# Expert outputs of a mixture-of-experts layer: a scatter by matmul per job, or a store per job and one gather per token

## Chip, cores and metric

The kernel runs on one core of one Trainium2 chip. The metric is the device time of one execution in microseconds (us). Before the change it is 1543.35 us, the median of three runs (1543.27 to 1545.74).

## What is computed

A decoder trunk of two layers on 256 tokens of 1024 channels, in float32. Layer 0 is a pooling and gating mixer, followed by a dense SwiGLU feed-forward (hidden size 2816). Layer 1 is an RWKV-7 time mixing, followed by the mixture of experts that the change touches; a last RMSNorm with a gain ends the kernel. The experts' part:

```python
def moe_swiglu(xn, router, wg, wu, wd):
    logits = xt.astype(F32) @ router.astype(F32)
    top_vals, top_idx = lax.top_k(logits, TOP_K)          # TOP_K = 2 of 8 experts
    top_w = jax.nn.softmax(top_vals, axis=-1)
    gates = jnp.sum(jax.nn.one_hot(top_idx, N_EXPERTS, dtype=F32) * top_w[..., None], axis=1)
    for e in range(N_EXPERTS):                            # D_FF_EXPERT = 3584
        out = out + gates[:, e:e + 1] * swiglu(xt, wg[e], wu[e], wd[e]).astype(F32)
```

## The kernel before

**Two halves of every weight.** Matrix products run in float32r with both factors split in a high and a low part. A weight piece of 128x1024 is copied to `w_hi` by ScalarE (L1635), and VectorE writes the rest, piece minus `w_hi`, to `w_lo` (L1731). TensorE then makes three products for each (L1531 to L1533). `w_hi` and `w_lo` hold four pieces each, so ScalarE writes piece n+4 only when TensorE has used piece n. The dense feed-forward of layer 0 does the same with `f_hi` (L2042) and `f_lo` (L2153).

**Jobs.** The router picks two experts for each token. Tokens are sorted by expert with a one-hot matrix and ranks; an expert with more than 128 tokens gets a second job, so there are 8 to 11 jobs, and the trace has 8 (56 loads of each of the three weights, seven in a job). Job 0 is written out, the others run in a loop (`Fori(1, J)`) on each engine. A job takes up to 128 token rows, in slots of its own, and goes through seven chunks of 512 hidden columns: gate product, up product, SiLU times up, transposes (L1549), down product into PSUM banks 4 and 5. One chunk has three loads of 2 MB ("g", "u", "d"), 21 in a job, each in four pieces, so 84 pieces in a job. The names `i` and `j` in the code are the load within a job and the job.

**How rows get in.** The normed token rows are scattered once to a scratch tensor in memory, `expert_rows`, at row 128*expert + rank, by four indirect DMAs of GpSimd (L1919); `row_at` holds those rows. Each job reads its 128 rows from there (L1466), and TensorE turns them (L1567). The scratch is cleared at the start from `zero_rows`, 8 MB issued on SyncE (SP) after chunk 0 of the dense feed-forward (L1964).

**How outputs get out, before the change.** A job's output, 128x1024 in PSUM banks 4 and 5, is scaled by the gates of its rows and split in `Yhi` (ScalarE, L1653) and `Ylo` (VectorE, L1842). TensorE multiplies it by a one-hot matrix `PT` (8 products, L1579 and L1580, `scattered`), which gives 256 token rows in four banks, and VectorE adds these to `h` (four additions, L1835). This is done in the next job, behind its first gate product, and for the last job at the end. `PT` and the gates come from `Pg`, made by `onehot` on VectorE (L1818; for job 0 L1778), turned by two transposes on TensorE (L1594) and read at L1884 and L1885.

**Order around the change.** SP's loads of experts follow one another through a ring of seven slots; load i+7 waits until load i has been split (`free`). In the dense feed-forward SP loads 11 chunks of 3 MB through four slots. Chunk 3 waits for the first residual sum, and before chunk 4 SP runs `rwkv_lora_sp` (L549), which waits for the first clear (`x_clear`) and issues nine small loads. ScalarE starts on a chunk only when its three loads have all landed (L2039). At the end, ScalarE and VectorE take the norm of `h` and the rows are stored.

Of the kernel before, what the change touches and what calls it, by code (L numbers as in the profile page):

```python
# [105 lines left out]
def trunk(nc, I, cst_dram, cols_dram, out, stop=None):  # L106
    ctx = ExitStack()
    with ctx:
# [84 lines left out]
        n_r = sem("norm_recip")  # L193
        n_tr, n_eva, n_evd = sem("norm_transposed"), sem("norm_cols_act"), sem("norm_cols_dve")
        dvc = sem("dve_chain")
        acc_ = sem("act_chain")
        plc = sem("pool_chain")
        p_in, a_ev, g_ev = sem("in_proj"), sem("pool_in_copied"), sem("gelu_done")
        z_pad = sem("pads_zeroed")
        s_pooled, s_ymm, s_yev = sem("pooled"), sem("pool_mm"), sem("pool_out")  # L200
# [31 lines left out]
        f_phi, f_plo, f_pc = sem("ffn_pieces_hi"), sem("ffn_pieces_split"), sem("ffn_pieces_used")  # L232
        s_out = [sem(f"out{i}_written") for i in range(3)]

        chain = {"dve": 0, "act": 0, "pool": 0}
        CH = {"dve": dvc, "act": acc_, "pool": plc}

        def link(eng, which, ins):

# [309 lines left out]
        def rwkv_lora_sp(sp):  # L549
            sp.wait_ge(s_h, 4)  # L550
            sp.wait_ge(x_clear, 16)
            one = lambda name: I[name].rearrange("a (k p) n -> p (a k) n", p=P)
            two = lambda name: I[name].rearrange("a k n -> (a k) n")
            g2 = two("o_g2")
            for dst, src in ((w1s, one("o_w1")), (a1s, one("o_a1")), (g1s, one("o_g1")), (w2s[0:64, :], two("o_w2")),
                             (w2s[64:65, :], I["o_w0"]), (a2s[64:P, :], two("o_a2")), (g2a, g2[0:P, :]),
                             (g2b[0:32, :], g2[P:160, :]), (hspread, cst_dram[:, HSPREAD_AT:HSPREAD_AT + 1024])):
                sp.dma_start(dst, src).then_inc(lora_in, 16)
# [816 lines left out]
        def rwkv_pool(pool):  # L1375
# [19 lines left out]
        rows_dram = nc.dram_tensor("expert_rows", (2 * NE * P, D), F32).ap()  # L1395
        ng_in = sem("ffn_norm_gain_in")
        x_zero, x_clear, x_at, x_put, x_in = (sem(x) for x in (
            "zero_rows_set", "expert_rows_cleared", "row_index", "rows_scattered", "expert_rows_in"))
        zero_rows = wu(5, 1024, 1024)
        rows_in = xn[:, 0:D]  # L1400
        spare = xnT[:, :, :].rearrange("p k t -> p (k t)")
# [42 lines left out]
        def moe_sp(sp):  # L1444
            sp.wait_ge(o_mm, 56)
            sp.dma_start(router, I["o_router"].rearrange("a (k p) e -> p (a k) e", p=P)).then_inc(r_w, 16)
            wg = I["o_moe_wg"].rearrange("a e (k p) f -> (a e) p k f", p=P)
            wup = I["o_moe_wu"].rearrange("a e (k p) f -> (a e) p k f", p=P)
            wd = I["o_moe_wd"].rearrange("a e (k p) n -> (a e) p k n", p=P)

            def load(i, e):
                what, c = LOADS[i]
                if what == "d":
                    src = wd[bass.ds(e, 1), :, 4 * c:4 * c + 4, :]
                    dst = slot(SLOTS[i % 7]).rearrange("p (k n) -> p k n", k=4)
# [12 lines left out]
            def free(i, j):  # L1468

                sp.wait_ge(m_lo, j * NP + 4 * (i + 1))  # L1470

            for i in range(NL):
                if i == 0:
                    sp.wait_ge(l_xu, lev(1, 1, 1))
                if i == 1:
                    sp.wait_ge(t_u, 4)
                if i == 2:
                    sp.wait_ge(t_y, 4)
                if i == 4:
                    sp.wait_ge(gn_sp, 2)  # L1480
                    sp.wait_ge(wo_done, 4)
                if i >= 7:
                    free(i - 7, 0)
                load(i, 0)
                if i == 14:
                    sp.wait_ge(r_jobs, 2)
                    sp.dma_start(gain, I["final_norm"].partition_broadcast(P)).then_inc(r_in, 16)
                    sp.wait_ge(x_put, 64)
                    rows(0)
            J = sp.value_load(jobs[0:1, 12:13], min_val=NE, max_val=NE + 3)  # L1490
            with sp.Fori(1, J) as j:
                e = sp.value_load(jobs[0:1, bass.ds(j + 16, 1)], min_val=0, max_val=NE - 1)
                for i in range(NL):
                    free(i - 7, j)
                    load(i, e)
                    if i == 14:
                        rows(j)

# [9 lines left out]
        def moe_pe(pe):  # L1508
# [60 lines left out]
                    if k % 4 == 3:  # L1569
                        last.then_inc(m_ga, 1)  # L1570

            def scattered(j):

                pe.wait_ge(m_pte, j)
                pe.wait_ge(m_yl, j * 2)
                for b in range(TB):
                    for q in range(2):
                        dst = psum[:, 6 - 2 * q + b, :]
# [4 lines left out]
            def job(j, first):  # L1583
                pe.wait_ge(m_xg, j + 1)
                for c in range(NEC):
                    hidden(j, 0, c)
                    if c == 0 and not first:
                        scattered(j)
                    if c == 1:
                        if not first:  # L1590
                            pe.wait_ge(s_h, j * 4 + 12)
                        pe.wait_ge(m_pg, j + 1)
                        for b in range(TB):
                            last = nc.tensor.transpose(psum[:, 7, b * P:(b + 1) * P], Pg[:, b * P:(b + 1) * P], ident)  # L1594
                        last.then_inc(m_pt, 1)
# [5 lines left out]
                    if c == NEC - 1:  # L1601
                        down(j, c - 1, (0, 1))
                        turned(j, c)
                        down(j, c - 1, (2, 3))
                    elif c >= 1:
                        down(j, c - 1)
                down(j, NEC - 1)

# [2 lines left out]
            J = pe.value_load(jobs[0:1, 12:13], min_val=NE, max_val=NE + 3)  # L1611
            with pe.Fori(1, J) as j:
                job(j, False)
            scattered(J)

        def moe_act(act):
            act.wait_ge(gn_sp, 2)
# [31 lines left out]
            def outputs(j):  # L1649

                act.wait_ge(m_pc, j * NP)
                for q in range(2):
                    nc.scalar.activation(Yhi[:, 512 * q:512 * q + 512], psum[:, 4 + q, :], ACT.Copy,  # L1653
                                         scale=gate).then_inc(m_yc, 1)
# [25 lines left out]
            with act.Fori(1, J) as j:  # L1680
                job(j, False)
            root_table()
            outputs(J)
            for b in range(TB):
                for q in range(2):
                    act.wait_ge(s_h, J * 4 + (9 + 2 * b + q))
                    n = 2 * b + q
                    nc.scalar.activation(xn3[:, b, 512 * q:512 * q + 512], h[:, b, 512 * q:512 * q + 512], ACT.Square,
                                         accum_out=small[:, 104 + n:105 + n]).then_inc(n_ss, 1)
# [29 lines left out]
        def moe_dve(dve):  # L1719
# [54 lines left out]
            go(V.tensor_tensor(oh2, oh2, wide("w2"), ALU.mult))  # L1774
            V.tensor_tensor(gt[:, :, NE:2 * NE], oh1, oh2, ALU.add)
            go(V.tensor_tensor(gt[:, :, 0:NE], oh1, oh2, ALU.add))
            for b in range(TB):
                last = V.tensor_scalar(Pg[:, b * P:(b + 1) * P], C("iota"), rk[:, b, 0:1], gt[:, b, 0:1], ALU.is_equal, ALU.mult)  # L1778
            last.then_inc(m_pg, 1)

            A_, B_, O_ = tb_["ova"], tb_["ovb"], tb_["ovc"]

# [43 lines left out]
                                           xg_split[:, 0, 4 * q:4 * q + 4, :].bitcast(F32), ALU.subtract)  # L1826
                last.then_inc(m_xg, 1)

            def scattered(j, o=0):

                for b in range(TB):
                    for q in range(2):
                        dve.wait_ge(m_sc, j * 4 + (4 * o + 2 * b + q - 3))
                        hs = h[:, b, 512 * q:512 * q + 512]
                        V.tensor_tensor(hs, hs, psum[:, 6 - 2 * q + b, :], ALU.add).then_inc(s_h, 1)  # L1835

            def outputs(j, o=0):

                dve.wait_ge(m_xg, j + (o + 1))
                for q in range(2):  # L1840
                    dve.wait_ge(m_yc, j * 2 + (2 * o + q - 1))
                    V.scalar_tensor_tensor(out=Ylo[:, 512 * q:512 * q + 512], in0=psum[:, 4 + q, :], scalar=gate,  # L1842
                                           in1=Yhi[:, 512 * q:512 * q + 512].bitcast(F32), op0=ALU.mult,
                                           op1=ALU.subtract).then_inc(m_yl, 1)
# [6 lines left out]
            def job(j, first):  # L1851
# [7 lines left out]
                for i, (what, c) in enumerate(LOADS):  # L1859
# [8 lines left out]
                        pieces_lo(j, i, (1, 2, 3))  # L1868
                    elif not first or i > 0:
                        pieces_lo(j, i)  # L1870
                    if i == 0 and not first:
                        outputs(j)
                    if (what, c) == ("u", 0) and not first:
                        scattered(j)
                    if (what, c) == ("u", 1) and first:
                        job_list()
                    if what == "u" and c >= 1:
# [1 line left out]

                    if i >= 1 and LOADS[i - 1][0] == "u" and LOADS[i - 1][1] < NEC - 1:  # L1880
                        gated(LOADS[i - 1][1])
                    if (what, c) == ("d", 1):
                        dve.wait_ge(m_pt, j + 1)
                        V.tensor_reduce(gate, psum[:, 7, 0:256], AX.X, ALU.add)  # L1884
                        V.tensor_scalar(PT[:, :], psum[:, 7, 0:256], 0.0, None, ALU.is_gt).then_inc(m_pte, 1)  # L1885
                    if (what, c) == ("d", 3):
                        nxt = dve.value_load(jobs[0:1, bass.ds(j + 1, 1)], min_val=0, max_val=2 * NE - 1)
                        onehot(nxt)

            job(0, True)  # L1890
            J = dve.value_load(jobs[0:1, 12:13], min_val=NE, max_val=NE + 3)
            with dve.Fori(1, J) as j:
                job(j, False)
            last_job = dve.value_load(jobs[0:1, 13:14], min_val=NE - 1, max_val=NE + 2)
            outputs(last_job, 1)
            scattered(last_job, 1)

            dve.wait_ge(r_in, 16)
            for b in range(TB):
# [14 lines left out]
        def moe_pool(pool):  # L1914
# [3 lines left out]
            for i in range(2 * TB):  # L1918
                nc.gpsimd.indirect_dma_start(rows_dram, bass.IndirectOffsetOnAxis(row_at[:, i:i + 1], 0), xn3[:, i % TB, :],  # L1919
                                             None).then_inc(x_put, 16)  # L1920
        y_done = sem("y_done")


# [3 lines left out]
        def _(sp):  # L1927
# [16 lines left out]
            for c in range(NFC):  # L1944
# [17 lines left out]
                if c == 0:  # L1962
                    sp.wait_ge(x_zero, 1)
                    sp.dma_start(rows_dram.rearrange("(n p) d -> p n d", p=P),  # L1964
                                 zero_rows.unsqueeze(1).to_broadcast([P, 2 * NE, D])).then_inc(x_clear, 16)
            if reached(3):
                rwkv_sp(sp)
                wo_sp(sp)
# [415 lines left out]
```

## Time and profile before

| | us |
|---|---|
| Median of three runs | 1543.35 |
| Profiled execution, first to last instruction (span) | 1541.7 |
| What lies outside the span, by the median | 1.65 |
| TensorE busy | 1512.7 (98%) |
| VectorE busy | 1268.4 (82%) |
| ScalarE busy | 1009.2 (65%) |
| GpSimd busy | 9.3 (1%) |

The profile is of one execution. PE is TensorE, PEld its weight loads, DVE VectorE, ACT ScalarE, POOL GpSimd, SP SyncE, and a q behind a name its sequencer. Times in its rows are microseconds from the first instruction. The granted clock is a share of TensorE's full 2.4 GHz, so 0.50 is 1.2 GHz. "DMA share" is the mean busy share of the 16 DMA engines, slightly over 1 where packets overlap. "Busy" of a matmul includes its pipeline, so the distance from one start to the next is what a matmul costs.

### The profile page before, as it was taken

Reading aid. Unit: us, or ns where it says so; the run is one execution under the profiler, and the core shown is the slowest. Engines: PE = TensorE matmul, PEld = TensorE weight load, DVE = VectorE, ACT = ScalarE, POOL = GpSimd, SP = SyncE. Lnnn points to the kernel's source line nnn. Section 1 sums busy time; section 2 is a strip of 40 time slices with the busy share of each in tenths; the row PEclk is TensorE's granted clock in tenths of the full one; section 3 lists DMA queues with packets and bytes.
Section 4 is the critical chain, followed back from the end, with each engine's and each line's share of the span. In section 5 each row is a group of like instructions: output and inputs, shape, how many; then the busy total and the mean of one; then the engine's idle time right before and its main releaser. Section 6 shows DMA issues by size and latency. Waiting matters only on the chain.

```text
span 1541.7 us, 21572 instructions
## 1 busy us (share of the span) xinstructions
PE 1512.7 (98%) x7854; PEld 1265.2 (82%) x7854; DVE 1268.4 (82%) x1442; ACT 1009.2 (65%) x1154; POOL 9.3 (1%) x10
## 2 busy tenths in 40 slices
PE   8999999999999999999999999999999999999997
PEld 5788888799899677888888888888888888888885
DVE  3756666767875269999999999999999999999997
ACT  3444444653523157878887888887878888887886
POOL 0000000000000010000000000000000000000000
PEclk9999999999999999999999999999999999999999
DMA  9789443034004479999999999999999999999970
GB/s 361 309 268 298 164 164 109 0 110 136 1 1 165 178 266 396 397 375 357 386 365 361 386 363 362 387 359 360 384 381 345 379 381 348 376 380 347 375 288 27
DMA packets 203269, 439.36 MB, mean 285 GB/s; under 512 B 7217, under 2 KB 44337, under 8 KB 203090
## 3 DMA queue, kind: packets, MB, share of 16 engines
q1 hardware_dynamic: 200434, 434.05, 77.0%
q10 hardware_dynamic: 2208, 2.50, 0.5%
q0 software_dynamic: 576, 2.10, 0.3%
q8 instruction: 36, 0.59, 0.2%
q14 instruction: 15, 0.12, 0.0%
HBM read 427.09 MB, written 11.53 MB: 285 GB/s over the span
## 4 chain that ended last, share of the span: by engine, by line
PE 95%; DVE 3%; ACT 1%; issue 1%; DMA 0%; DVEq 0%; ACTq 0%
PE psum L1531 20%; PE psum L1533 19%; PE psum L1532 19%; PE psum L2313 5%; PE psum L590 5%; PE psum L2315 3%; PE psum L2237 2%; PE psum L879 2%; PE psum L2277 2%; PE psum L2279 2%; PE psum L2278 2%; PE psum L1549 2%; PE psum L775 1%; PE psum L765 1%; PE psum L680 1%; PE psum L2230 1%
## 5 line engine op out<-in xcount | busy, mean ns | idle before, releaser
L1731 DVE TENSOR_TENSOR w_lo<-ring,w_hi 128x1024 fp32r<-128x1024 f32 x672 | 805.5, 1224 | 51.3 <-ACT w_hi L1635 11.0
L1635 ACT ACTIVATE w_hi<-ring 128x1024 fp32r<-128x1024 f32 x672 | 711.4, 1062 | 187.0 <-PE psum L1533 186.9
L1531 PE MATMUL psum<-w_hi,xg_split 128*128 128x512 f32 x896 | 353.6, 395 | 0.4 <-DVE xg_split L1825 0.4
L1533 PE MATMUL psum<-w_lo,xg_split 128*128 128x512 f32 x896 | 349.5, 390 | 0.0
L1532 PE MATMUL psum<-w_hi,xg_split 128*128 128x512 f32 x896 | 348.9, 389 | 0.0
L1533 PEld LDWEIGHTS psum<-w_lo,xg_split 128*128 128x128 f32 x896 | 168.2, 188 | 35.7
L1531 PEld LDWEIGHTS psum<-w_hi,xg_split 128*128 128x128 f32 x896 | 168.3, 188 | 34.1 <-DVE xg_split L1825 0.6
L1532 PEld LDWEIGHTS psum<-w_hi,xg_split 128*128 128x128 f32 x896 | 168.5, 188 | 33.5
L1531 PE MATMUL psum<-w_hi,ht_split 128*128 128x512 f32 x448 | 176.2, 393 | 1.7 <-DVE w_lo L1731 1.7
L1533 PE MATMUL psum<-w_lo,ht_split 128*128 128x512 f32 x448 | 174.6, 390 | 0.0
L1532 PE MATMUL psum<-w_hi,ht_split 128*128 128x512 f32 x448 | 174.4, 389 | 0.0
L2313 PE MATMUL psum<-x_split,f_hi 128*128 128x512 f32 x352 | 125.1, 399 | 0.8 <-DVE x_split L357 0.4
L2153 DVE TENSOR_TENSOR f_lo<-ring,f_hi 128x1024 fp32r<-128x1024 f32 x66 | 79.5, 1223 | 52.0 <-ACT f_hi L2042 52.0
L2042 ACT ACTIVATE f_hi<-ring 128x1024 fp32r<-128x1024 f32 x66 | 69.0, 1056 | 53.6 <-PE psum L2315 31.3
L1531 PEld LDWEIGHTS psum<-w_hi,ht_split 128*128 128x128 f32 x448 | 84.1, 188 | 21.1 <-issue 4.0
L2315 PE MATMUL psum<-x_split,f_lo 128*128 128x256 f32 x352 | 98.9, 281 | 0.0
L1533 PEld LDWEIGHTS psum<-w_lo,ht_split 128*128 128x128 f32 x448 | 84.1, 188 | 17.8
L1532 PEld LDWEIGHTS psum<-w_hi,ht_split 128*128 128x128 f32 x448 | 84.2, 188 | 17.0
L2313 PEld LDWEIGHTS psum<-x_split,f_hi 128*128 128x128 f32 x352 | 66.1, 188 | 17.7 <-DVE f_lo L2153 0.7
L2315 PEld LDWEIGHTS psum<-x_split,f_lo 128*128 128x128 f32 x352 | 66.5, 189 | 0.4
L590 PE MATMUL psum<-mixed_parts,time_mix_parts 128*128 128x256 f32 x448 | 64.5, 283 | 0.0
L590 PEld LDWEIGHTS psum<-mixed_parts,time_mix_parts 128*128 128x128 f32 x448 | 58.5, 192 | 0.1
(365 smaller groups left out, 1589.8 us busy)
## 6 DMA issues: line engine op xcount, KB each, us to landing
ring<-o_moe_wg_dram SPq DMA_DIRECT2D x56, 2048.0 KB, 8.7
ring<-o_moe_wu_dram SPq DMA_DIRECT2D x56, 2048.0 KB, 9.0
ring<-o_moe_wd_dram SPq DMA_DIRECT2D x56, 2048.0 KB, 8.9
ring<-e_ffn_wg_dram SPq DMA_DIRECT2D x11, 1024.0 KB, 5.6
ring<-e_ffn_wu_dram SPq DMA_DIRECT2D x11, 1024.0 KB, 8.2
ring<-e_ffn_wd_dram SPq DMA_DIRECT2D x11, 1024.0 KB, 11.0
expert_rows<-work SPq DMA_DIRECT2D x1, 8192.0 KB, 28.7
ring<-e_w_in_dram SPq DMA_DIRECT2D x2, 2048.0 KB, 18.2
```

What stands on the lines that cost most here:

```text
L590: last = nc.tensor.matmul(psum[0:rows, n % 8, 0:width], l, r, start=(i == 0), stop=(i == len(lhs_rhs) - 1))
L879: return nc.tensor.matmul(psum[:, n, :], YT[:, k, (n // 2) * P:(n // 2 + 1) * P], wo_s[n % 2][:, k, :], start=(k == 0), stop=(k == KT - 1))
L1531: nc.tensor.matmul(dst, x_hi, hi, start=first, stop=False)
L1532: nc.tensor.matmul(dst, x_lo, hi, start=False, stop=False)
L1533: return nc.tensor.matmul(dst, x_hi, lo, start=False, stop=last_)
L1549: last = nc.tensor.transpose(psum[:, 6, f * P:(f + 1) * P], SIL[c % 2][:, f * P:(f + 1) * P], ident)
L1635: nc.scalar.activation(w_hi[:, (4 * i + n) % 4, :], piece(i, n), ACT.Copy).then_inc(m_hi, 1)
L1731: V.tensor_tensor(w_lo[:, r, :], piece(i, n), w_hi[:, r, :].bitcast(F32), ALU.subtract).then_inc(m_lo, 1)
L2042: nc.scalar.activation(as_piece(f_hi, i, what), ffn_piece(what, c, n), ACT.Copy).then_inc(f_phi, 1)
L2153: nc.vector.tensor_tensor(as_piece(f_lo, i, what), ffn_piece(what, c, n), as_piece(f_hi, i, what).bitcast(F32), ALU.subtract).then_inc(f_p ...
L2313: nc.tensor.matmul(r3(psum[:, bank, :], 2), hi[:, k, :], x_split[:, 0:2, k, :], start=(k == 0), stop=False)
L2315: last = nc.tensor.matmul(psum[:, bank, T:2 * T], lo[:, k, :], x_split[:, 1, k, :], start=False, stop=(k == KT - 1))
```

## The change

Each job's output is copied without its gates to `y_rows` (the upper half of `xn`) by ScalarE and stored by SP to a new scratch `expert_out`, at the job's own rows, while the next job runs. `expert_out` is cleared like `expert_rows`, 8 MB more, issued behind chunk 3 of the dense feed-forward; `rwkv_lora_sp` waits for that too. Scatter, one-hot and gate transposes stay for the last job alone. For all other jobs, GpSimd fetches two rows for each token by four indirect DMAs, when 15 of the 21 loads of the last job have been split. It then multiplies each by its weight and adds it to `h`: four multiplications and four additions, of 128x1024 each. The last job's rows in `expert_out` are still zero, so that nothing is added twice. VectorE's last additions to `h` wait for GpSimd's.

```diff
@@ rwkv_lora_sp
             sp.wait_ge(x_clear, 16)
+            sp.wait_ge(y_put, 16)
@@ names
+        y_dram = nc.dram_tensor("expert_out", (2 * NE * P, D), F32).ap()
+        y_put, y_add = sem("expert_out_written"), sem("expert_out_added")
+        y_rows = xn[:, D:2 * D]
+        y_tok = slot(3).rearrange("p (c n) -> p c n", c=2 * TB)
@@ moe_sp, loop over jobs
                     load(i, e)
+                    if i == 9:
+                        sp.wait_ge(m_yc, j * 2)
+                        at = sp.value_load(jobs[0:1, bass.ds(j - 1, 1)], min_val=0, max_val=2 * NE - 1)
+                        dst = y_dram.rearrange("(n p) d -> n p d", p=P)[bass.ds(at, 1), :, :]
+                        sp.dma_start(dst.rearrange("o p d -> (o p) d"), y_rows).then_inc(y_put, 16)
@@ moe_pe, job
                     hidden(j, 0, c)
-                    if c == 0 and not first:
-                        scattered(j)
-                    if c == 1:
-                        if not first:
-                            pe.wait_ge(s_h, j * 4 + 12)
-                        pe.wait_ge(m_pg, j + 1)
+                    if c == 5 and first:
+                        pe.wait_ge(m_pg, 1)
                         for b in range(TB):
                             last = nc.tensor.transpose(psum[:, 7, b * P:(b + 1) * P], Pg[:, b * P:(b + 1) * P], ident)
...
                     elif c >= 1:
+                        if c == 1 and not first:
+                            pe.wait_ge(m_yc, j * 2)
                         down(j, c - 1)
...
-            scattered(J)
+            scattered()
@@ moe_act
             def outputs(j):
+                act.wait_ge(m_pc, j * NP)
+                act.wait_ge(y_put, j * 16)
+                for q in range(2):
+                    nc.scalar.activation(y_rows[:, 512 * q:512 * q + 512], psum[:, 4 + q, :], ACT.Copy).then_inc(m_yc, 1)
+
+            def outputs_gated(j):
...
-            outputs(J)
+            outputs_gated(J)
@@ moe_dve
-            for b in range(TB):
-                last = V.tensor_scalar(Pg[:, b * P:(b + 1) * P], C("iota"), rk[:, b, 0:1], gt[:, b, 0:1], ALU.is_equal, ALU.mult)
-            last.then_inc(m_pg, 1)
...
-            def scattered(j, o=0):
+            def scattered():
                 for b in range(TB):
+                    dve.wait_ge(y_add, 4 * b + 5)
                     for q in range(2):
-                        dve.wait_ge(m_sc, j * 4 + (4 * o + 2 * b + q - 3))
+                        dve.wait_ge(m_sc, 2 * b + q + 1)
...
-                    if i == 0 and not first:
-                        outputs(j)
-                    if (what, c) == ("u", 0) and not first:
-                        scattered(j)
...
-                    if (what, c) == ("d", 1):
-                        dve.wait_ge(m_pt, j + 1)
+                    if (what, c) == ("d", 4) and first:
+                        dve.wait_ge(m_pt, 1)
...
-                    if (what, c) == ("d", 3):
-                        nxt = dve.value_load(jobs[0:1, bass.ds(j + 1, 1)], min_val=0, max_val=2 * NE - 1)
-                        onehot(nxt)
+                    if (what, c) == ("d", 3) and first:
+                        at = dve.value_load(jobs[0:1, 13:14], min_val=NE - 1, max_val=NE + 2)
+                        onehot(dve.value_load(jobs[0:1, bass.ds(at, 1)], min_val=0, max_val=2 * NE - 1))
@@ moe_pool
+            pool.wait_ge(r_jobs, 2)
+            last_job = pool.value_load(jobs[0:1, 13:14], min_val=NE - 1, max_val=NE + 2)
+            pool.wait_ge(y_put, last_job * 16 + 16)
+            pool.wait_ge(m_lo, last_job * NP + 4 * 15)
+            nc.gpsimd.tensor_tensor(small[:, 502:504], tb_["w1"], tb_["w2"], ALU.add).then_inc(y_add, 1)
+            pool.wait_ge(y_add, 1)
+            for i in range(2 * TB):
+                nc.gpsimd.indirect_dma_start(y_tok[:, i, :], None, y_dram,
+                                             bass.IndirectOffsetOnAxis(row_at[:, i:i + 1], 0)).then_inc(x_put, 16)
+            pool.wait_ge(x_put, 128)
+            for b in range(TB):
+                for n, w in enumerate(("w1", "w2")):
+                    y = y_tok[:, n * TB + b, :]
+                    nc.gpsimd.tensor_scalar(y, y, tb_[w][:, b:b + 1], None, ALU.mult).then_inc(y_add, 1)
+                    pool.wait_ge(y_add, 4 * b + 2 * n + 2)
+                    nc.gpsimd.tensor_tensor(h[:, b, :], h[:, b, :], y, ALU.add).then_inc(y_add, 1)
+                    if n == 0:
+                        pool.wait_ge(y_add, 4 * b + 3)
@@ sync, loads of the dense feed-forward
+                if c == 3:
+                    sp.dma_start(y_dram.rearrange("(n p) d -> p n d", p=P),
+                                 zero_rows.unsqueeze(1).to_broadcast([P, 2 * NE, D])).then_inc(y_put, 16)
```

## Rows read from the trace of the kernel before

**Rows 1.** The page, part 1: busy time, share of the span, instructions.

```profile
PE 1512.7 (98%) x7854; PEld 1265.2 (82%) x7854; DVE 1268.4 (82%) x1442; ACT 1009.2 (65%) x1154; POOL 9.3 (1%) x10
```

**Rows 2.** Waits, whole span: engine, line, releaser: total us, times, longest.

```profile
ACT w_hi L1635 <- PE psum L1533: 186.9, 579, 2.6
```

**Rows 3.** Busy us by engine, granted clock, DMA share, GB/s: job 0, a loop job.

```profile
588.00:667.00 79.00, 78.84 (x359) 65.38 (x360) 75.22 (x72) 62.35 (x64) 0.00 (x0) 1.00 1.04 395
...
908.00:1029.00 121.00, 121.00 (x555) 100.18 (x553) 114.59 (x111) 97.53 (x103) 0.00 (x0) 1.00 1.00 370
```

**Rows 4.** The chain that ended last, experts' stage: start us, us, what.

```profile
560.65 0.61 DVE xnT L1778 x2
...
1028.95 0.87 PE psum L1567 x8
...
1149.16 0.44 PE psum L1549 x4
1149.60 0.87 PE psum L1567 x8
...
1511.65 0.87 PE psum L1567 x8
```

**Rows 5.** Timeline of PE, job 1's scatter: start us, us, operation.

```profile
690.06 0.39 PE L1579 MATMUL psum<-y_hi,onehot_T 128*128 128x512 f32 x1
...
691.87 0.39 PE L1531 MATMUL psum<-w_hi,xg_split 128*128 128x512 f32 x1
```

**Rows 6.** Groups by line: busy us, mean ns | idle before.

```profile
L1731 DVE TENSOR_TENSOR w_lo<-ring,w_hi 128x1024 fp32r<-128x1024 f32 x672 | 805.5, 1224 | 51.3 <-ACT w_hi L1635 11.0
...
L1835 DVE TENSOR_TENSOR h<-h,psum 128x512 f32<-128x512 f32 x32 | 19.8, 683 | 0.8 <-PE psum L1580 0.8
```

**Rows 7.** Timeline of SP: dense feed-forward, then the end of a loop job.

```profile
99.20 3.87 SPq L1961 DMA_DIRECT2D ring<-e_ffn_wd_dram  x1
...
110.98 0.37 SPq L558 DMA_DIRECT2D work<-o_w_dram  x1
...
120.51 4.26 SPq L1961 DMA_DIRECT2D ring<-e_ffn_wd_dram  x1
...
1009.02 0.39 SPq L1459 DMA_DIRECT2D ring<-o_moe_wg_dram  x1
```

**Rows 8.** DMA issues: KB, us to landing: clear; chunk 3; chunk 4.

```profile
expert_rows<-work SPq DMA_DIRECT2D x1, 8192.0 KB, 28.7
...
ring<-e_ffn_wd_dram SPq DMA_DIRECT2D x1, 1024.0 KB, 12.4
...
ring<-e_ffn_wd_dram SPq DMA_DIRECT2D x1, 1024.0 KB, 12.7
```

**Rows 9.** As rows 3, PE alone: around TensorE's idle spell; during the first clear.

```profile
55.00:65.00 10.00, 7.84 (x29) 0.83 1.03 421
50.00:55.00 5.00, 5.00 (x25) 1.00 1.02 419
```

**Rows 10.** Timelines, layer 0: idle spell of PE; ACT, then PE, at chunk 4.

```profile
58.72 0.48 PE L2277 MATMUL psum<-x_split,fh_split 128*128 128x512 f32 x1 [2.16 <-DVE out_parts L2136]
...
141.51 2.16 ACT L2042 ACTIVATE f_hi<-ring 128x1024 fp32r<-128x1024 f32 x2
...
150.66 0.39 PE L2313 MATMUL psum<-x_split,f_hi 128*128 128x512 f32 x1
```

**Rows 11.** POOL: groups (busy us, mean ns); landing of L1919's DMAs; their first in time.

```profile
L1919 POOL DMA_INDIRECT expert_rows<-xn,row_at x4 | 7.2, 1811 | 145.0 <-DVE xg_split L1825 144.1 <-issue 0.9
L1376 POOL MEMSET work<- 128x1024 f32 x1 | 1.0, 951 | 0.3 <-POOLq L2370 0.3
...
DMA to landing us min/median/max: 10.7/11.1/11.5
...
564.50 2.34 POOL L1919 DMA_INDIRECT expert_rows<-xn,row_at  x1 [144.07 <-DVE xg_split L1825]
```

**Rows 12.** Timeline of DVE, end of the kernel: last job's additions to h.

```profile
1532.52 2.48 DVE L1835 TENSOR_TENSOR h<-h,psum 128x512 f32<-128x512 f32 x4 [0.82 <-PE psum L1580]
```

More of the change, by code:

```diff
@@ L195, in trunk @@
         dvc = sem("dve_chain")
-        acc_ = sem("act_chain")
-        plc = sem("pool_chain")
         p_in, a_ev, g_ev = sem("in_proj"), sem("pool_in_copied"), sem("gelu_done")
@@ L233, in trunk @@
         s_out = [sem(f"out{i}_written") for i in range(3)]
-        chain = {"dve": 0, "act": 0, "pool": 0}
-        CH = {"dve": dvc, "act": acc_, "pool": plc}
+        chain = {"dve": 0}
+        CH = {"dve": dvc}
         def link(eng, which, ins):
@@ L1397, in trunk @@
         x_zero, x_clear, x_at, x_put, x_in = (sem(x) for x in (
-            "zero_rows_set", "expert_rows_cleared", "row_index", "rows_scattered", "expert_rows_in"))
+            "zero_rows_set", "expert_rows_cleared", "row_index", "expert_rows_moved", "expert_rows_in"))
+        y_dram = nc.dram_tensor("expert_out", (2 * NE * P, D), F32).ap()
+        y_put, y_add = sem("expert_out_written"), sem("expert_out_added")
+        y_rows = xn[:, D:2 * D]
+        y_tok = slot(3).rearrange("p (c n) -> p c n", c=2 * TB)
         zero_rows = wu(5, 1024, 1024)
@@ L1570, in rows_turned @@
                         last.then_inc(m_ga, 1)
-            def scattered(j):
-                pe.wait_ge(m_pte, j)
-                pe.wait_ge(m_yl, j * 2)
+            def scattered():
+                pe.wait_ge(m_pte, 1)
+                pe.wait_ge(m_yl, 2)
                 for b in range(TB):
@@ L1682, in moe_act @@
             root_table()
-            outputs(J)
+            outputs_gated(J)
             for b in range(TB):
                 for q in range(2):
-                    act.wait_ge(s_h, J * 4 + (9 + 2 * b + q))
+                    act.wait_ge(s_h, 13 + 2 * b + q)
                     n = 2 * b + q
@@ L1827, in gathered, with scattered, outputs @@
                 last.then_inc(m_xg, 1)
-            def scattered(j, o=0):
+            def scattered():
                 for b in range(TB):
+                    dve.wait_ge(y_add, 4 * b + 5)
                     for q in range(2):
-                        dve.wait_ge(m_sc, j * 4 + (4 * o + 2 * b + q - 3))
+                        dve.wait_ge(m_sc, 2 * b + q + 1)
                         hs = h[:, b, 512 * q:512 * q + 512]
                         V.tensor_tensor(hs, hs, psum[:, 6 - 2 * q + b, :], ALU.add).then_inc(s_h, 1)
-            def outputs(j, o=0):
-                dve.wait_ge(m_xg, j + (o + 1))
+            def outputs(j):
+                dve.wait_ge(m_xg, j + 2)
                 for q in range(2):
-                    dve.wait_ge(m_yc, j * 2 + (2 * o + q - 1))
+                    dve.wait_ge(m_yc, j * 2 + (q + 1))
                     V.scalar_tensor_tensor(out=Ylo[:, 512 * q:512 * q + 512], in0=psum[:, 4 + q, :], scalar=gate,
@@ L1894, in moe_dve @@
             last_job = dve.value_load(jobs[0:1, 13:14], min_val=NE - 1, max_val=NE + 2)
-            outputs(last_job, 1)
-            scattered(last_job, 1)
+            outputs(last_job)
+            scattered()
             dve.wait_ge(r_in, 16)
```

## The prediction, made before the changed kernel was run

> **What bounds the kernel now.** I read the page's first part, the table of waits, the busy time of each engine by stretch, and then the chain that ended last, through the experts' stage. TensorE is busy for 98% of the span [rows 1]. In a loop job it is busy for the whole of 121 us at full clock, with VectorE at 114.59, ScalarE at 97.53 and the DMA engines at a share of 1.00 with 370 GB/s [rows 3]. All three look full, so the waits decide. The long one is ScalarE's for TensorE, 186.9 us before it may overwrite a piece [rows 2]. The supply of pieces thus waits for TensorE; VectorE waits little for ScalarE, 11.0 us in all [rows 6]. The chain runs on TensorE from job to job: the eight turns of the next job's rows stand at 1028.95 and 1149.60 [rows 4], a period of 120.65 us, and in 121 us of TensorE time none is idle. What leaves TensorE in a job is gained whole, as long as VectorE (second, 95% full) and the DMA engines keep up.
>
> **Removed from TensorE.** The scatter's eight products run from 690.06 to the next product at 691.87, 1.81 us [rows 5]. Four transposes take 0.44 us on the chain [rows 4], so the two of the gates take 0.22. Both leave each of the seven loop jobs: 7 x (1.81 + 0.22) = 14.2 us. Job 0 keeps its two transposes, later. Job 0's two one-hot instructions at L1778 stand on the chain before its first product, 0.61 us [rows 4]; they go too, and what follows is the work that was next anyway. Removed: 14.8 us. The last job's scatter stays. This could be more only if those products also cost stalls, and the uninterrupted start-to-start spacing (1.81/8 = 0.226 us) says not.
>
> **Removed from VectorE.** In each loop job four additions of 683 ns [rows 6], and by the nearest rows two instructions for `Ylo` at about the same price, two small one-hots and the two reads of the turned gates: 2.7 + 1.4 + 1.5, some 5.6 us. VectorE goes to 114.6 - 5.6 = 109 us in a period of 118.6, so it has about 8% free instead of 5%. This costs or gives nothing by itself, because TensorE sets the pace. ScalarE does two copies as before, at the same place; its new wait for the last store is old by then, and the new wait on TensorE before the first down product asks for those copies, issued a whole product earlier.
>
> **Added stores and SP.** One value load and one 512 KB store in each loop job, behind load 9. What stands behind it on SP is load 10, which waits for a split that comes later anyway. A job then moves 21 x 2.10 + 0.52 in + 0.52 out = 45.1 MB in 118.6 us, 380 GB/s. The busy share says full at 370, but with more queued the same engines moved 395 [rows 3], so I take zero, with a rival for it. Even a small lack is covered for long, since a load is issued seven loads (some 40 us) ahead of its use.
>
> **The second clear.** This is the part with a place on the path. Chunk 3's last load is issued at 99.20 and lands 12.4 later, at 111.6 [rows 7, 8]. The new 8.39 MB queue behind it. The first clear moved at 419 GB/s when alone [rows 9], which is 20.0 us, so the second lands at about 131.6. SP now waits for it before the nine small loads, which began at 110.98 [rows 7]: 20.6 us late. Chunk 4's last load lands at 120.51 + 12.7 = 133.2 now [rows 7, 8], so at about 153.8. ScalarE needs all of chunk 4 for its first piece. It took it as the second of the two copies from 141.51, some 11 us before that, and TensorE used it at 150.66 [rows 10]. With one copy (1.06, half of about 2.16) and one split (1.22) behind the landing, TensorE starts chunk 4 at 156.1: a stall of 5.4 us. Afterwards the chunks that follow are late by less than their slack, since SP issues them without a wait. TensorE's clock pays too. After 2.16 us without work in the earlier part [rows 10] the granted clock was 0.83 over ten microseconds [rows 9], that is for a third of them at the lower of the two levels, 1.2 GHz instead of 2.4, a loss of 1.7 us. I add it once: 7.1 us. Below, the bound is 0 (the lag of 11 us absorbs it, if the clear shares the engines instead of standing in the way); above, with the full 28.7 us that the first clear took from issue to landing [rows 8], it is 7.1 + 8.7 = 15.8.
>
> **GpSimd's end work.** Load 15 of the last job (i=14) has been split when SP could issue the load that reuses its slot. In a loop job that was 1009.02, 19.9 us before the turns at 1028.95 [rows 4, 7]; in the last one it is 1511.65 - 19.9 = 1491.7. The output store of the job before is long done. Four indirect DMAs took 7.2 us of GpSimd with small gaps, 8.1 in all, and each landed in 11.1 us [rows 11]; the last is issued some 6.2 us after the first and lands between 1502 and 1510 (earlier, since no loads run any more). Then come four one-input and four two-input operations of 128x1024. No row shows such an operation on GpSimd. The nearest is a write-only fill of the same size, 0.951 us [rows 11], and I take that for one input and twice it for two: 4 x 0.95 + 4 x 1.9 = 11.4 us. Below, 8 x 0.95 = 7.6; above, 8 x 2.34 (the first indirect DMA's span on that engine [rows 11]) = 18.7. The result is needed at 1532.52, where the additions for the last job start [rows 12]: from 1508, 11.4 us of work leave over 10 us, so as a chain of its own it costs nothing.
>
> But VectorE works in just this stretch, and its main work, `w_lo` = piece - `w_hi`, reads two SBUF tensors, 1.224 us each [rows 6]. If such an instruction and GpSimd's cannot run together, VectorE loses GpSimd's whole 11.4 us. Over the some 21 us that eight operations in turn with eight splits take, VectorE has 8% free, 1.7 us, and four buffers less a copy and a split give 4 x 1.36 - 1.36 - 2.3 = 1.8 us of lead. TensorE then stands 11.4 - 3.5 = 7.9 us, between 0 (they don't collide, or only in part) and 18.7 - 3.5 = 15.2. The trace can't say: no GpSimd operation that reads SBUF ran before. I take 7.9, for a reason of structure: both engines would read two streams at one time beside everything else.
>
> The Trainium skill, "SBUF — State Buffer", section "Who interferes with whom", speaks against this change here: a VectorE instruction with two SBUF inputs contends with a GpSimd instruction that reads SBUF, and the second to start blocks until the first is done. No row here tests it; by it the term is the 7.9 above, without it 0. The skill's "GPSIMD Engine Reference", section "Elementwise — side-by-side cycle accounting", has about 2.6 cycles an element for a two-input addition, which as an estimate is 2.2 us for 1024; the sum would then be about 1.2 us worse.
>
> **Sum.** -14.8 + 7.1 + 7.9 = +0.2 us on a span of 1541.7. With the 1.65 us between span and median this gives 1543.6 us, no change. A measurement of this kernel tells 0.2% (3.1 us) from no change.
>
> **Rivals.**
> A. GpSimd's operations run beside VectorE's splits without slowing them. For it: an indirect DMA of GpSimd already runs beside VectorE's splits, and the splits there keep their 1.22 us. Against it: those DMAs don't read two tiles. Then 1543.35 - 14.8 + 7.1 = 1535.7.
> B. The second clear is hidden, by faster loads of chunk 4 or an earlier clear. For it: 11 us between ScalarE's need and TensorE's. Against it: the queue order, worked out above. With the rest as forecast, 1543.6 - 7.1 = 1536.5.
> C. The other side: GpSimd's chain ends after the last product and the additions to `h` wait. It begins to cost when the eight operations, with their waits between splits, take over 1532.5 - 1508 = 24.5 us, 3.1 us each, 3.3 times the fill. At 5 us each they take 40, end 15.5 us late, and VectorE's splits get their time back only in part; with half of the 7.9: 1543.35 - 14.8 + 7.1 + 15.5 + 4 = 1555.2. For it: if VectorE keeps the port, GpSimd gets in only between splits. Against it: the spans on that engine here go to 2.34 us [rows 11].
> D. The DMA engines become the bound, if 371 GB/s is all they give in this pattern: 45.1 MB take 121.6 us, 3 us more than 118.6 in each of six jobs less the lead of the ring. This takes back at most the 14.2, after 30 us of lead are used; so it costs little here, up to 5 us: 1549. Against it: 395 GB/s in job 0.
>
> **How the numbers follow.** Forecast 0.47, A 0.30, B 0.07, C 0.11, D 0.05. The forecast's own range is 1538 to 1549 (stall at chunk 4 from 4 to 10, GpSimd's operations 8 to 15 us): of its 0.47 some 0.30 lie within 0.2%, 0.09 below and 0.08 above. A is faster in 0.27 and the same in 0.03. B is faster. C is slower in 0.09, the same in 0.02; D is slower. So faster 0.43, same 0.35, slower 0.22. For 8 in 10 the range goes from 1533.5 (A with a stall of 5) to 1551 (the forecast with a slow GpSimd, D); C's far end and A with B together (1528.6) are left out.
>
> **What would show it.** Turns of the next job's rows (L1567) 118.6 us apart. SP's nine small loads starting near 131.6, TensorE idle some 5 us before chunk 4, and a granted clock below 1 just after. In the last 30 us: GpSimd's first multiplication between 1500 and 1510 of the old time; VectorE's splits longer than 1.22 us, or gaps between them of GpSimd's length, with TensorE waiting for `w_lo`, or, by rival A, splits unchanged. By rival C, VectorE's additions to `h` wait for GpSimd. The prediction is wrong in its mechanism if the splits keep their spacing while GpSimd computes, or if chunk 4 starts on time.

## The result, and the profile after

The changed kernel takes 1547.22 us (median of 20 runs), the kernel before 1543.75 us beside it: a ratio of 1.0019, 95% interval 1.0014 to 1.0025, so 2.9 us slower (2.2 to 3.9); the medians themselves are 3.5 apart. The forecast was 1543.6 us, no change, within a range of 1533.5 to 1551.0. The profiled execution has a span of 1546.0 us, 4.3 more than before.

The page after, busy time (as [rows 1] before) and the chain's shares, then the chain's shares before:

```profile
PE 1505.3 (97%) x7784; PEld 1256.4 (81%) x7784; DVE 1251.1 (81%) x1370; ACT 1005.9 (65%) x1154; POOL 40.0 (3%) x23
...
PE 89%; DVE 3%; DMA 3%; SPq 2%; issue 1%; ACT 1%; DVEq 0%; ACTq 0%
```

```profile
PE 95%; DVE 3%; ACT 1%; issue 1%; DMA 0%; DVEq 0%; ACTq 0%
```

TensorE has 7.4 us less to do, yet its share of the chain is 89% instead of 95%. What came in its place stands in the line after: DMA 3% and SP's sequencer 2%, which were 0 before. That is the second clear and the issues and the load behind it.

**The gain is there.** The chain from job to job (start, us, what), two turns before, then three after, and a window of one loop job after (columns of [rows 3]):

```profile
666.94 0.87 PE psum L1567 x8
...
1390.94 0.87 PE psum L1567 x8
```

```profile
676.85 0.87 PE psum L1575 x8
795.39 0.87 PE psum L1575 x8
...
1388.57 0.87 PE psum L1575 x8
```

```profile
914.00:1033.00 119.00, 119.00 (x546) 98.49 (x544) 110.86 (x101) 97.19 (x103) 0.00 (x0) 1.00 1.01 375
```

Six periods take 711.72 us, 118.62 each, where they took 724.00. That is 2.05 less in each and 12.28 in all. TensorE is still never idle, and the DMA engines, with half a MB more to move in less time, keep pace at 375 GB/s. VectorE is busy for 110.86 us of such a window, 3.7 less than before.

**First place where it goes back: chunk 4 of the dense feed-forward.** SP's timeline after ([rows 7] before):

```profile
100.33 3.87 SPq L1987 DMA_DIRECT2D ring<-e_ffn_wd_dram  x1
104.24 0.71 SPq L1993 DMA_DIRECT2D expert_out<-work  x1
132.55 0.37 SPq L557 DMA_DIRECT2D work<-o_w_dram  x1
...
143.50 3.95 SPq L1987 DMA_DIRECT2D ring<-e_ffn_wd_dram  x1
```

Between the clear's issue and the first small load SP does nothing for 28 us. TensorE's first product of chunk 4, and the ten microseconds around it (busy us by engine, clock, DMA share, GB/s):

```profile
158.40 0.76 PE L2342 MATMUL psum<-x_split,f_hi 128*128 128x512 f32 x1 [6.86 <-DVE f_lo L2182]
```

```profile
156.00:166.00 10.00, 7.60 (x31) 6.62 (x32) 8.29 (x8) 5.53 (x6) 0.00 (x0) 0.66 1.08 364
```

TensorE was idle for 6.86 us in front of that product, where the kernel before had hardly any [rows 10]. The clock then averages 0.66 over ten microseconds, from which the part before the product counts for nothing; seen in two-microsecond windows, TensorE works at 0.50 (1.2 GHz) from 158.4 to some 163, which loses 2.2 us.

**Second place: the last 30 us.** GpSimd's timeline after (start, us, line, operation, idle before and who ended it):

```profile
1492.08 1.06 POOL L1936 DMA_INDIRECT ring<-expert_out,row_at  x1 [0.30 <-issue]
1497.78 3.18 POOL L1942 TENSOR_SCALAR ring<-ring,small 128x1024 f32<-128x1024 f32 x1 [4.64 <-DMA ring<-expert_out,row_at]
1501.04 2.65 POOL L1944 TENSOR_TENSOR h<-h,ring 128x1024 f32<-128x1024 f32 x1
1503.78 4.76 POOL L1942 TENSOR_SCALAR ring<-ring,small 128x1024 f32<-128x1024 f32 x1
1508.62 2.66 POOL L1944 TENSOR_TENSOR h<-h,ring 128x1024 f32<-128x1024 f32 x1
...
1522.75 2.38 POOL L1944 TENSOR_TENSOR h<-h,ring 128x1024 f32<-128x1024 f32 x1
```

VectorE's splits in the same stretch, one by one:

```profile
1498.74 1.54 DVE L1744 TENSOR_TENSOR w_lo<-ring,w_hi 128x1024 fp32r<-128x1024 f32 x1
1500.21 1.21 DVE L1744 TENSOR_TENSOR w_lo<-ring,w_hi 128x1024 fp32r<-128x1024 f32 x1
1501.34 3.43 DVE L1744 TENSOR_TENSOR w_lo<-ring,w_hi 128x1024 fp32r<-128x1024 f32 x1
1504.69 1.21 DVE L1744 TENSOR_TENSOR w_lo<-ring,w_hi 128x1024 fp32r<-128x1024 f32 x1
1505.83 2.05 DVE L1744 TENSOR_TENSOR w_lo<-ring,w_hi 128x1024 fp32r<-128x1024 f32 x1
1507.80 1.21 DVE L1744 TENSOR_TENSOR w_lo<-ring,w_hi 128x1024 fp32r<-128x1024 f32 x1
1508.94 3.42 DVE L1744 TENSOR_TENSOR w_lo<-ring,w_hi 128x1024 fp32r<-128x1024 f32 x1
```

Each addition of GpSimd (1501.04, 1508.62) meets a split of 3.4 us instead of 1.22 [rows 6]. A multiplication meets at most one of 2.05, and others of 1.21 run beside it. Over all eight operations the splits take 10.2 us more than 1.22 each. From the last full turn (1388.57) to the end there are 157.43 us, against 150.76 (1390.94 to 1541.7). As this stretch too is rid of one scatter (2.05), the end work costs 8.7 us in this execution.

### The profile page after: what moved, and what is told of

Same layout as the page of the kernel before. It is cut to its first block, busy times and chain, and to the rows that moved or that the text cites. A ratio compares the mean times of both kernels' runs of the same rounds, so it can differ in the third digit from the quotient of the medians.

```text
span 1546.0 us, 21362 instructions
## 1 busy us (share of the span) xinstructions
PE 1505.3 (97%) x7784; PEld 1256.4 (81%) x7784; DVE 1251.1 (81%) x1370; ACT 1005.9 (65%) x1154; POOL 40.0 (3%) x23
## 4 chain that ended last, share of the span: by engine, by line
PE 89%; DVE 3%; DMA 3%; SPq 2%; issue 1%; ACT 1%; DVEq 0%; ACTq 0%
PE psum L1539 19%; PE psum L1541 19%; PE psum L1540 19%; PE psum L589 5%; PE psum L2342 3%; DMA expert_out<-work 2%; PE psum L2266 2%; PE psum L878 2%; PE psum L2344 2%; DVE w_lo L1744 2%; PE psum L1557 1%; PE psum L2306 1%; PE psum L2308 1%; PE psum L2307 1%; PE psum L2259 1%
## 5 line engine op out<-in xcount | busy, mean ns | idle before, releaser
L1744 DVE TENSOR_TENSOR w_lo<-ring,w_hi 128x1024 fp32r<-128x1024 f32 x672 | 821.5, 1238 | 62.9 <-ACT w_hi L1641 16.0
L1540 PEld LDWEIGHTS psum<-w_hi,ht_split 128*128 128x128 f32 x448 | 84.9, 189 | 17.3
## 6 DMA issues: line engine op xcount, KB each, us to landing
ring<-o_moe_wg_dram SPq DMA_DIRECT2D x56, 2048.0 KB, 10.2
```

What stands on the lines that cost most here:

```text
L1540: nc.tensor.matmul(dst, x_lo, hi, start=False, stop=False)
L1744: V.tensor_tensor(w_lo[:, r, :], piece(i, n), w_hi[:, r, :].bitcast(F32), ALU.subtract).then_inc(m_lo, 1)
```

## The experiments

All times are medians, ratios are against the kernel before run beside it (1543.6 to 1544.1 us). "Faster" and "slower" in us follow from the ratio; the medians differ from that by up to 1.6 us. The changed kernel did not run in these series, so a difference to its 1547.22 us has a further uncertainty of some tenths. Each trace is of one execution. E1 and E6 leave out most of the sum over the gathered rows.

**E1: GpSimd's end operations made tiny.**

```diff
-                    y = y_tok[:, n * TB + b, :]
+                    y = y_tok[:, n * TB + b, 0:2]
-                    nc.gpsimd.tensor_tensor(h[:, b, :], h[:, b, :], y, ALU.add)...
+                    nc.gpsimd.tensor_tensor(h[:, b, 0:2], h[:, b, 0:2], y, ALU.add)...
```

> The changed kernel with GpSimd's eight operations at the end cut from 128x1024 to 128x2; it leaves out most of the sum over the gathered rows. Theory (the operations hold up VectorE's splits, and TensorE waits for them): the last stretch gets back some 8.7 us, so 1538.5 us, and VectorE's splits there are 1.22 us each again. Rival (the gathers, or the stores, hold up the last job, not the operations): it stays within 2 us of 1547.2.

1538.25 us, ratio 0.9964 (0.9953 to 0.9976). That is 9.0 us under the changed kernel's median. Gathers and stores are still there, and all splits take 1.21 to 1.23 us (ns min/median/max):

```profile
L1744 DVE TENSOR_TENSOR w_lo<-ring,w_hi x88: 1211/1225/1233, 1399.1 to 1521.7; 128x1024 fp32r<-128x1024 f32 x88
```

So it is the operations. In the traces, the stretch from the last full turn to the end is 149.24 us here (1388.86 to 1538.1) against 157.43, so 8.2 us shorter.

**E2: the second clear as a copy of the first, in the time mixing.**

```diff
-                if c == 3:
-                    sp.dma_start(y_dram..., zero_rows...).then_inc(y_put, 16)
@@ rwkv_lora_sp
-            sp.wait_ge(y_put, 16)
@@ rwkv_sp, at its end
+            sp.dma_start(y_dram, rows_dram).then_inc(y_put, 16)
@@ moe_pool
             pool.wait_ge(x_clear, 16)
+            pool.wait_ge(y_put, 16)
```

> The changed kernel, but expert_out is cleared by one memory-to-memory DMA from the already cleared expert_rows, issued in the time mixing, where the DMA engines move almost nothing; SP waits for no clear before chunk 4. Theory (the second clear stalls chunk 4 and lowers the clock after it): 9.2 us less, so 1538 us, and chunk 4 starts without idle time of TensorE. Rival (a stall that would come at another place anyway, or a copy that disturbs the time mixing): less than 3 us gained.

1540.05 us, ratio 0.9975 (0.9964 to 0.9985): 7.2 us under the changed kernel, less than the 9.2 expected. SP's timeline shows the nine small loads back at their place, and the copy at 379.54:

```profile
111.79 0.37 SPq L556 DMA_DIRECT2D work<-o_w_dram  x1
...
379.54 0.61 SPq L568 DMA_DIRECT2D expert_out<-expert_rows  x1
```

Where the other 2 us are can be read from one later mark, SP's first load of the time mixing's second matrix. It stands 8.96 us earlier than in the changed kernel for the first matrix (245.37 against 254.33), but only 7.22 earlier for the second (323.87 against 331.09). In between, the granted clock falls once in the kernel before (and in E2, 0.93 over 300 to 324), and not in the changed kernel. The kernel before, then the changed kernel, each at its own time:

```profile
299.00:323.00 24.00, 24.00 (x124) 20.61 (x124) 20.29 (x26) 20.39 (x39) 0.00 (x0) 0.93 0.00 1
```

```profile
309.00:331.00 22.00, 21.98 (x122) 19.15 (x121) 19.54 (x25) 19.66 (x37) 0.00 (x0) 1.00 0.00 1
```

0.07 of 24 us is the 1.7 us. E1 and E3, which also stall at chunk 4, don't have this fall. But neither have the traces of E4 and E8, which don't stall there (1.00 over 300 to 324 in E8), so the stall isn't shown to be what prevents it.

**E3: the second clear alone, on the kernel before.** The diff adds the tensor `expert_out`, the clear behind chunk 3 and SP's wait, as the change has them.

> The kernel before, with only the second 8 MB clear added behind chunk 3 and SP's wait for it. Theory: chunk 4's loads land some 21 us later, TensorE idles 6.9 us and runs some 4.6 us at half clock, so 9 us slower than before: 1552.8 us. By the prediction's own numbers 7.1 us: 1550.8 us. Rival: the stall is due to something else in the change, and this is within 2 us of before.

1550.6 us, ratio 1.0045 (1.0032 to 1.0059), 6.9 us slower (4.9 to 9.1): the prediction's own 7.1, not the 9 that the trace of the changed kernel had suggested. The wait, by the waits of TensorE (total us, times, longest), is 6.5 us long, and at 299 to 323 the clock is 1.00 here too:

```profile
PE psum L2317 <- DVE f_lo L2157: 6.9, 2, 6.5
```

**E4: GpSimd's eight operations alone, on the kernel before.**

```diff
+            pool.wait_ge(m_lo, last_job * NP + 4 * 16)
...
+            for n in range(4):
+                y, z = y_tok[:, n, :], y_tok[:, (n + 1) % 4, :]
+                nc.gpsimd.tensor_scalar(y, y, tb_["w1"][:, 0:1], None, ALU.mult).then_inc(y_add, 1)
+                pool.wait_ge(y_add, 2 * n + 2)
+                nc.gpsimd.tensor_tensor(z, z, y, ALU.add).then_inc(y_add, 1)
+                pool.wait_ge(y_add, 2 * n + 3)
```

> The kernel before, with only eight GpSimd operations of the changed kernel's size (four multiplications, four additions, 128x1024 each, on a ring slot that nobody uses any more) in the last job, from the split of its 16th load. No gathers. Theory (GpSimd's reads and VectorE's splits exclude each other): some 8 to 9 us slower than before, 1552.3 us, with splits of 2 to 5 us. Rival (GpSimd alone doesn't matter; the gathers or TensorE's changed order do): within 1.5 us of before, splits of 1.22 us.

1551.24 us, ratio 1.0056 (1.0038 to 1.0075), 8.6 us slower (5.9 to 11.6), with splits of 3.42 and 2.05 us as in the changed kernel. The single executions spread from 1548.4 to 1556.8 us, and the traced one is the fastest (mean granted clock 0.998, against 0.992 in the slowest). No gather, no changed order of TensorE is needed for it.

**E5: 24 fills in their place.** The loop of E4 becomes `nc.gpsimd.memset(y_tok[:, n % 4, :], 0.0)`, 24 times.

> The kernel before, with 24 GpSimd fills of 128x1024 (0.95 us each, one after the other, some 24 us) in the last job, in the stretch where the reading operations stood; they write SBUF and read none. Theory (it is GpSimd's reading of SBUF that shuts out VectorE's splits of two SBUF inputs): VectorE's splits stay at 1.22 us and the time is within 1 us of before, 1543.6 us. Rival (any SBUF access of GpSimd does it, each for its length): splits of 2 us and more, and over 5 us slower.

1543.43 us, ratio 1.0001 (0.9990 to 1.0013). GpSimd's timeline, and the duration of all splits (ns min/median/max):

```profile
1497.04 24.30 POOL L1928 MEMSET ring<- 128x1024 f32 x24
```

```profile
L1731 DVE TENSOR_TENSOR w_lo<-ring,w_hi x672: 1210/1225/1229, 554.0 to 1525.8; 128x1024 fp32r<-128x1024 f32 x168
```

24 us of writing beside the splits lengthen none of them.

**E6: E1 and E2 together.**

> The changed kernel with the clear by copy and with GpSimd's eight operations cut to 128x2 (it leaves out most of the sum over the gathered rows). Theory (the two costs stand apart and nothing else of the change costs anything): the whole of the removed 14.8 us shows, 1528.8 us. Rival (the costs cover each other, or the stores and gathers have a price of their own): 1533 us or more.

1531.63 us, ratio 0.9909 (0.9895 to 0.9924): 14.1 us faster (11.7 to 16.2); by the medians it is 12.5. The time lies between the theory's 1528.8 and the rival's 1533 us, and the interval takes in the expected 14.8 less 0.6 (below). It is 15.6 us under the changed kernel, where E1 and E2 alone gave 9.0 and 7.2, so the two costs stand apart to within 0.6. That the stores and gathers cost nothing at all is not shown to better than the interval.

**E7: the eight operations behind the last output,** where VectorE rests (E4's loop after `pool.wait_ge(y_done, 3)`), executed once.

> The kernel before, with GpSimd's eight operations run behind the last output row, where VectorE does nothing. The span grows by their own length. Theory (in the last job they took 2.4 to 4.9 us each, because they waited for VectorE's splits too): alone some 1.2 us for a multiplication and some 2.3 us for an addition, so 14 us in all. Rival (they are that slow by themselves): 3 to 4.8 and 2.65 us, 28 us in all.

1563.25 us. Groups of GpSimd (busy us, mean ns | idle before):

```profile
L1926 POOL TENSOR_SCALAR ring<-ring,small 128x1024 f32<-128x1024 f32 x4 | 11.4, 2848 | 966.7 <-DVE h L1912 966.4
L1928 POOL TENSOR_TENSOR ring<-ring 128x1024 f32<-128x1024 f32 x4 | 9.4, 2339 | 0.3
```

Neither holds as a whole: the addition is 2.34 us as the theory had it, the multiplication 2.85 us, well over its 1.2, and all eight take 20.8 us, between its 14 and the rival's 28. In the last job a multiplication grew to up to 4.89 us, and an addition to 2.66: both sides wait for each other.

**E9 and E10: eight multiplications, or eight additions,** in E4's loop instead of four and four.

> The kernel before, with eight GpSimd multiplications by a column (one SBUF tensor in, 128x1024) in the last job and no additions. Theory (a multiplication shuts VectorE's splits out for some 0.8 us of its 2.85, an addition for 2.2 of its 2.34): VectorE loses under 6 us, spread over more than 30 us, of which its free time takes nearly all; splits of at most some 2 us, and the time within 3 us of before. Rival (any reading operation shuts them out for its whole length): 8 x 2.85 = 22.8 us lost, 15 us slower or more.

1546.16 us, ratio 1.0015 (1.0006 to 1.0024), 2.3 us slower (0.9 to 3.7). Three splits, with a shorter instruction of VectorE between the second and the third:

```profile
1500.51 1.22 DVE L1731 TENSOR_TENSOR w_lo<-ring,w_hi 128x1024 fp32r<-128x1024 f32 x1
1501.65 2.06 DVE L1731 TENSOR_TENSOR w_lo<-ring,w_hi 128x1024 fp32r<-128x1024 f32 x1
1504.22 1.21 DVE L1731 TENSOR_TENSOR w_lo<-ring,w_hi 128x1024 fp32r<-128x1024 f32 x1
```

> The kernel before, with eight GpSimd additions (two SBUF tensors in, 128x1024) in the last job and no multiplications. Theory: each lengthens one split to 3.4 us; VectorE loses 8 x 2.2 = 17.6 us, less some 3.5 us of free time and lead: 14 us slower than before. Rival (the loss goes by the count of operations or their spans, so like four and four): 8 us.

1558.59 us, ratio 1.0090 (1.0076 to 1.0104), 13.9 us slower (11.7 to 16.1). Two successive splits, and GpSimd's eight additions, 25.66 us together:

```profile
1502.59 3.41 DVE L1731 TENSOR_TENSOR w_lo<-ring,w_hi 128x1024 fp32r<-128x1024 f32 x1
1505.92 3.40 DVE L1731 TENSOR_TENSOR w_lo<-ring,w_hi 128x1024 fp32r<-128x1024 f32 x1
```

```profile
1499.18 25.66 POOL L1929 TENSOR_TENSOR ring<-ring 128x1024 f32<-128x1024 f32 x8
```

With additions alone eight successive splits take 2.8 to 3.4 us: each waits for nearly a whole addition. The cost follows the kind of operation: an addition takes up to 2.2 us from VectorE, a multiplication, although it is the longer one, about 0.8 at most.

**E8: a better version.** E2's clear, GpSimd only gathers, and VectorE sums behind the loop:

```diff
+                go(V.scalar_tensor_tensor(out=h[:, b, :], in0=y_tok[:, n * TB + b, :], scalar=w[:, b:b + 1], in1=h[:, b, :],
+                                          op0=ALU.mult, op1=ALU.add))
...
+            dve.wait_ge(x_put, 128)
+            added(0, 0)
+            added(0, 1)
+            added(1, 0)
             outputs(last_job)
             scattered()           # with added(1, 1) between the additions for b = 0 and b = 1
```

> The changed kernel with the clear by copy, and with the sum over the gathered rows on VectorE behind the loop: four instructions h = row * weight + h of 128x1024, some 1.3 us each, three of them while VectorE waits for the last job's output (3.2 us idle there), one between the additions for the two blocks of tokens. GpSimd only gathers. Theory: the 14.8 us less some 2 us on the path at the end, 1530.8 us, faster than both kernels. Rival (at the end every microsecond of VectorE is on the path): 5.2 us, 1534 us.

1533.09 us, ratio 0.9925 (0.9911 to 0.9938): 11.6 us faster than the kernel before (9.6 to 13.7). It beats both. The theory's gain of 12.8 us and the rival's of 9.6 both lie in that interval, so the trace has to decide. VectorE's timeline:

```profile
1509.15 3.91 DVE L1842 SCALAR_TENSOR_TENSOR h<-ring,small,h 128x1024 f32<-128x1024 f32 x3
1513.30 1.41 DVE L1860 SCALAR_TENSOR_TENSOR y_lo<-psum,small,y_hi 128x512 fp32r<-128x512 f32 x2 [0.23 <-DVE h L1842]
...
1516.80 1.28 DVE L1842 SCALAR_TENSOR_TENSOR h<-ring,small,h 128x1024 f32<-128x1024 f32 x1
```

Three of the four fill the wait for the last output. From the last turn to the end there are 32.27 us (1493.83 to 1526.1) against 30.05 before: 2.2 us, of 5.2 that the four take, and so the theory's 2. The traced execution is the fastest of five, 1527.95 us: its clock has none of the early falls of the others (1.00 over 55 to 65 and over 300 to 324), and they lie outside of this stretch.

## Why the prediction held, and where it didn't

**Removed, 14.8 us.** Right to within 0.6: seven times 2.05 are 14.3 by the turns, and E6 has 14.1 in all (12.5 by the medians). The 0.61 for job 0's one-hots was wrong. What follows it was already due: the chain now runs through TensorE's 32 products that pick out job 0's rows, ScalarE's copy of the result and one split of it. So from SP's first expert load (499.25) to GpSimd's first scatter of the rows (572.59) are 73.34 us, where there were 73.39. The next thing late was as late.

**VectorE, ScalarE, the stores, SP.** Nothing, as said; rival D fell with 375 GB/s and no idle time in the loop. VectorE got rid of 3.7 us in a loop job and not of 5.6, so it has 7% free instead of 8%.

**The second clear, 7.1 us.** The mechanism was right in each step: small loads at 132.55 (131.6 forecast, in a run that is 0.94 us late at the residual sum), chunk 4 late, idle time, then half the clock. The two terms were a little small, 6.86 for 5.4 and 2.2 for 1.7, and 1.7 came back later by a clock spell that stayed away, so that the sum (6.9 by E3, 7.2 by E2) is the forecast's. That agreement is partly luck. Rival B fell: 11 us of lag do not hide 20.

**GpSimd's end work, 7.9 us.** That the operations and the splits exclude each other was right, and the cost was 8.6 to 9.0 (E4, E1). The step "VectorE loses GpSimd's whole time" holds for additions only, so that the 7.9 came near is partly luck: two sizes in it were wrong and made up for each other. A multiplication takes 2.85 us alone, three times the 0.95 taken from the fill; but it shuts the splits out for at most 0.8 of that, so the 0.95 was near the time that VectorE loses. An addition has 2.34 instead of 1.9. With the real durations, 20.8 us, the step as written would have given 17.3, twice what was measured. What counts is the sum that the splits show, 10.2 us. The 3.5 of relief was too large: of the 10.2, 8.2 reached the end of the kernel (the traces of E1 and the change), so 2.0 were absorbed. Half clock in the last scatter, whose eight products stand 0.43 us apart instead of 0.23, is no part of this, since they stand 0.43 apart in E1 too. Rival A is refuted by E1, E4 and E10. Rival C did not occur: GpSimd ended at 1525.1, 11 us ahead of the additions to `h` at 1536.13. Its gathers landed in 5.7 us, not in the 11.1 of [rows 11]; they ran at the end of the loads and behind them.

The Trainium skill's "SBUF — State Buffer", section "Who interferes with whom", is borne out by E4, E5 and E10: reads of GpSimd collide with two-input instructions of VectorE, fills don't. Its rule that the second blocks until the first is done agrees for additions (3.4 us splits) up to some 0.15 us, but not for multiplications, beside which splits of 1.21 us ran (E9).

**Why it came out slower and not the same.** -14.1, +6.9 and +8.6 make +1.4 with intervals of some 2 us each, and the measured interval begins at 2.2. The two traces, 4.3 us apart, can be added up: 0.9 of late start ahead of the change, +6.9 and +2.2 at chunk 4, -1.7 for the fall of the clock that stayed away, +1.8 for a clock spell in job 0 (0.91 over 580 to 600), -12.3 in the loop and +6.7 from the last turn on, which makes 4.5. The late start is no effect of the change (E10, the same code there, has it, and E8 doesn't). E1 and E2 also have the spell in job 0, and the kernel before hasn't. E6, with the same job 0, has one of about the same size some 30 us earlier in its work (columns of [rows 3]), and the traced execution of E8 has none:

```profile
555.00:560.00 5.00, 5.00 (x33) 5.00 (x33) 2.98 (x17) 3.68 (x5) 0.00 (x0) 0.66 1.02 398
```

So whether it belongs to the change stays open. Beyond the single traces, the changed kernel runs at a lower clock on the whole: the mean granted clock is 0.991 to 0.994 in its 20 executions, and 0.996 in most of the kernel before. The difference is worth some 5 us as an estimate (0.003 of 1546), of which a part falls where TensorE waits anyway.

## What to carry to other kernels

Before work goes to an idle engine, ask whether it reads SBUF beside two-input instructions of a VectorE that is nearly full; a fused multiply-add on VectorE in a wait that exists anyway cost 2.2 us where GpSimd's eight operations cost 8.6. A large setup DMA costs where the next load queues behind it, so put it in a stretch in which the DMA engines rest, from a source that is already there. A saving inside a loop (14 us here) can be eaten by two single events outside of it, so follow each new wait and transfer to the thing behind it.

## What was not expected of the hardware

GpSimd's multiplication by a column is slower alone (2.85 us for 128x1024) than its addition of two tensors (2.34 us), yet disturbs VectorE far less (0.8 against 2.2 us for each). Small operations aren't free: of 128x2 they still took 0.3 to 1.4 us beside the splits in E1. And TensorE's clock makes single losses of 1.7 to 2.2 us that come and go between executions of like code. 2.16 us of idle [rows 10] were followed by half clock in the kernel before. In E4's trace, whose code is the same up to the last job, the same 2.16 us stand in the same place and the clock stays at 1.00 over 55 to 65 (PE's columns of [rows 9]):

```profile
55.00:65.00 10.00, 7.84 (x35) 1.00 1.02 419
```

1.9 us of idle in job 0 were followed by half clock in some traces and not in others. A difference of 2 us between two single traces can be this alone.
